# A token and memory block: x and memory loaded with channels in partitions as well, and 1/rms applied after the projections

## The reference, cut to what matters

```python
def rms_norm(x, g):
    y = xf * lax.rsqrt(jnp.mean(xf * xf, axis=-1, keepdims=True) + EPS)
    return (y * g).astype(x.dtype)

def hybrid_mixer(xn, ...):                      # xn = rms_norm(x, norm_mix)
    x_lru, g_lru, q, k, v = split(xn @ w_in)    # five times 512 columns
    xc = causal_depthwise_conv(x_lru, conv_w, conv_b)
    y_lru = rg_lru(xc, w_rg, b_rg, w_ig, b_ig, lru_lambda) * gelu(g_lru)
    y_att = attention(rope(q), rope(k), v)      # 8 heads, causal
    return concatenate([rms_norm(y_lru), rms_norm(y_att)]) @ w_out

def memory_cross_attention(hn, mem, ...):
    q = hn @ w_xq
    k, v = split(rms_norm(mem, norm_mem) @ w_xkv)
    ...
h = x + hybrid_mixer(...); h = h + memory_cross_attention(...); h = h + hier_moe(...)
```

## Time and profile before

| | us |
|---|---|
| three runs: median (lowest to highest) | 689.82 (687.18 to 691.67) |
| profiled execution: span from first to last instruction | 689.8 |
| PE busy | 551.7 (80%) |
| DVE busy | 225.3 (33%) |
| ACT busy | 168.8 (24%) |
| DMA, mean over the span | 345 GB/s |
| projections (up to the first expert) | about 0 to 240 |
| experts | about 240 to 680 |

### The profile page before, as it was taken

One profiled execution on the slowest core, in us unless ns is written; L12 is line 12 of the kernel. 1 busy time (PEld: TensorE's weight loads), 2 busy tenths in 40 slices (PEclk: granted clock), 3 DMA queues, 4 the chain that ended last, 5 costly groups with the idle time before them and its releaser, 6 DMA issues.

```text
span 689.8 us, 11578 instructions
## 1 busy us (share of the span) xinstructions
PE 551.7 (80%) x4768; PEld 346.0 (50%) x4768; DVE 225.3 (33%) x425; ACT 168.8 (24%) x325; POOL 40.1 (6%) x25
## 2 busy tenths in 40 slices
PE   3979999999999887868668767867777686767764
PEld 3968999789888644535224322522342252224221
DVE  3795888664653521222001110210120120112002
ACT  6557585463441111110000010010000000100002
POOL 2022351200000000000000000000000000000000
PEclk9989999999999999999657855976795587679557
DMA  9846743497579889999999999999999999999993
GB/s 326 289 152 211 259 152 112 156 376 265 197 293 381 313 341 409 409 410 410 410 409 409 410 410 410 409 409 410 410 410 408 410 410 410 409 409 410 410 410 139
DMA packets 75941, 237.85 MB, mean 345 GB/s; under 512 B 3728, under 2 KB 16144, under 8 KB 75920
## 3 DMA queue, kind: packets, MB, share of 16 engines
q1 hardware_dynamic: 75920, 237.56, 88.7%
HBM read 236.49 MB, written 1.05 MB: 344 GB/s over the span
## 4 chain that ended last, share of the span: by engine, by line
SPq 54%; PE 30%; issue 4%; DVE 4%; DMA 3%; POOL 1%; ACT 0%; DVEq 0%; POOLq 0%
SPq L433 53%; PE psum L562 12%; PE psum L548 8%; DMA ring<-in_w_gate_up 3%; DVE work L1259 1%; PE psum L797 1%; PE psum L822 1%; PE psum L696 1%; PE psum L719 1%; PE psum L531 1%; DVE split_w L1181 1%; PE psum L745 1%; PE psum L781 1%; POOL stat L1106 1%; PE psum L591 1%
## 5 line engine op out<-in xcount | busy, mean ns | idle before, releaser
L797 PE MATMUL psum<-ring,xg 128*32 128x256 f32 x2048 | 166.5, 468 | 61.6 <-DMA ring<-in_w_gate_up 61.0
L797 PEld LDWEIGHTS psum<-ring,xg 128*32 128x32 f32 x2048 | 66.5, 126 | 154.5 <-DMA ring<-in_w_gate_up 110.5
L562 PE MATMUL psum<-split_w,split_act 128*128 128x512 f32 x432 | 104.6, 400 | 5.4 <-DVE split_w L1181 4.2
L822 PE MATMUL psum<-ring,small 128*32 128x256 f32 x1024 | 91.6, 519 | 12.9 <-ACT small L885 11.7
L562 PEld LDWEIGHTS psum<-split_w,split_act 128*128 128x128 f32 x432 | 82.1, 192 | 23.5 <-DVE split_w L1181 4.6
L1548 DVE SCALAR_TENSOR_TENSOR small<-small,psum 128x128 f32<-128x128 f32 x32 | 9.2, 288 | 202.7 <-ACT small L1070 202.7
L1070 ACT ACTIVATE small<-psum 128x128 f32<-128x128 f32 x32 | 8.9, 277 | 268.9 <-PE psum L797 268.9
L548 PE MATMUL psum<-split_act,split_w 128*128 128x256 f32 x576 | 70.1, 284 | 1.4 <-DVE split_act L1194 1.4
L885 ACT ACTIVATE split_w<-landing 128x2048 fp32r<-128x2048 f32 x30 | 57.3, 1914 | 56.5 <-PE psum L562 32.8
L548 PEld LDWEIGHTS psum<-split_act,split_w 128*128 128x128 f32 x576 | 69.5, 192 | 2.1 <-DVE split_w L1215 1.7
L1181 DVE TENSOR_TENSOR split_w<-landing,split_w 128x2048 fp32r<-128x2048 f32 x25 | 58.9, 2360 | 29.3 <-ACT split_w L885 29.3
(11 more groups left out here) (169 smaller groups left out, 348.3 us busy)
## 6 DMA issues: line engine op xcount, KB each, us to landing
ring<-in_w_gate_up SPq DMA_DIRECT2D x128, 1024.0 KB, 18.3
ring<-in_w_down SPq DMA_DIRECT2D x64, 1024.0 KB, 18.4
landing<-in_w_in SPq DMA_DIRECT2D x10, 1024.0 KB, 9.2
landing<-in_w_xkv SPq DMA_DIRECT2D x8, 1024.0 KB, 6.3
landing<-in_w_out SPq DMA_DIRECT2D x4, 1024.0 KB, 6.8
landing<-in_w_xq SPq DMA_DIRECT2D x4, 1024.0 KB, 5.3
landing<-in_w_xo SPq DMA_DIRECT2D x4, 1024.0 KB, 5.1
res<-in_x SPq DMA_DIRECT2D x2, 512.0 KB, 3.8
```

The source lines that it names most:

```text
L562: i = mm(b, src[t][:, k0 + k, P * h:P * h + P], w[a][:, k, :], start=first and k == 0 and n == 0, stop=last and k == CT - 1 and n == 2)
L797: i = mm(half[SLOTS * strip:SLOTS * strip + SLOTS], xg[:, CT * part + k, SLOTS * j:SLOTS * j + SLOTS], w[:, k, :, P * strip:P * strip + P] ...
L822: i = mm(bank(HY)[SLOTS * strip:SLOTS * strip + SLOTS, 0:256], hidT[:, SLOTS * k:SLOTS * k + SLOTS], w[:, k, 256 * strip:256 * strip + 256 ...
```

## The change

x and memory are also passed in with channels in partitions (`x_turned`, `mem_turned`; the laying out is part of the inputs' preparation). The kernel splits them right there with the gain, before any 1/rms is known. The 1/rms is a factor of each token, so it is applied when a projection leaves PSUM: where tokens are in partitions, as the scale of the copy (`scaled`); where channels are in partitions, by a multiplication on DVE with a row `bcx` or `bcm` that holds 1/rms of all tokens in each partition (`columns_scaled`). That row is made by PE from a diagonal matrix and a matrix of ones (`broadcast`, `diagonals`). The transposes Tx and Tm are gone. Weight half 0, its split and x come in three pieces (`FIRST_CHUNKS`). The parameters stand ahead of the constants in `early` and are loaded by themselves.

```diff
-JOBS += [(f"Tx{c}", 2) for c in range(4)]
 JOBS += [(f"xl{c}", 1) for c in range(2)]
-JOBS += [(f"Tm{c}", 2) for c in range(4)]
+JOBS += [("bcx", 1)]
 JOBS += [(f"q{h}", 1) for h in range(2)] + [(f"k{h}", 1) for h in range(2)]
...
+JOBS += [("bcm", 1)]
 JOBS += [(f"xk{c}", 1) for c in range(4)]
...
+            for n, (a, b) in enumerate(FIRST_CHUNKS):
+                sp.dma_start(xraw[:, a:b], x_turned[:, a:b]).then_inc(xT_loaded[n], 16)
+                if n == 0:
+                    sp.dma_start(ctab[:, 0:N_PARAMS], early[:, 0:N_PARAMS]).then_inc(params_loaded, 16)
+                sp.dma_start(raw(0, KC)[:, a:b], half_source(0)[:, a:b]).then_inc((w_first_loaded + raw_loaded)[n], 16)
+            load_half(1)
             for h in range(NH):
                 sp.dma_start(res[:, h], x_in[:, h]).then_inc(x_loaded[h], 16)
-            sp.dma_start(ctab, early).then_inc(early_loaded, 16)
-            load_half(0)
-            load_half(1)
-            sp.dma_start(memraw, mem_in).then_inc(mem_loaded, 16)
+            sp.dma_start(ctab[:, N_PARAMS:], early[:, N_PARAMS:]).then_inc(early_loaded, 16)
             load_half(2)
+            load_half(3)
+            sp.dma_start(mraw, mem_turned).then_inc(mT_loaded, 16)
             sp.dma_start(bd.rearrange("p c n -> p (c n)"), late[:, (KC + 1) * N_ROUTES:]).then_inc(bd_loaded, 16)
-            load_half(3)
+            sp.dma_start(memtok, mem_in).then_inc(mem_loaded, 16)
             sp.dma_start(latetab, late[:, 0:(KC + 1) * N_ROUTES]).then_inc(router_loaded, 16)
...
+            w, b = slot(0, KC), begin("xl0")
+            for part, (first, last) in enumerate(FIRST_CHUNKS):
+                pe.wait_ge(x_lo, part + 1)
...
+            channels(1, "xl1", xs_)
             pe.wait_ge(early_loaded, 16)
-            pe.wait_ge(normed_act, 1)
-            pe.wait_ge(normed_dve, 1)
-            turn("Tx", xtok)
-            channels(0, "xl0", xs_, "Tx")
-            channels(1, "xl1", xs_)
-            pe.wait_ge(normed_act, 2)
-            pe.wait_ge(normed_dve, 2)
-            turn("Tm", memraw)
+            pe.wait_ge(diag_ready, 1)
+            broadcast("bcx")
             tokens_whole(2, ["q0", "q1"], xs_)
             tokens_whole(4, ["k0", "k1"], xs_)
...
-            for c in range(4):
-                await_read(pe, f"Tm{c}")
+            pe.wait_ge(diag_ready, 2)
+            broadcast("bcm")
+            pe.wait_ge(m_lo, 1)
```

ACT no longer copies gl0, gl1, xk0 and xk2 out of PSUM; it copies q, k, v, xv0 and xv2 through `scaled`:

```diff
-            plain("gl0", gx[:, 0:2])
             split_hi(12)
-            plain("gl1", gx[:, 2:4])
+            await_fill(act, "bcm")
+            release(copy(bcm, pb("bcm")[:, 0:S]), "bcm")
```

On POOL the second half of weight half 0 is gone:

```diff
             for stage in (1, 2):
                 pool.wait_ge(meansq, stage)
                 power(2 * (stage - 1), 2, rstd)
-                if stage == 1:
-                    pool.wait_ge(w_hi, 1)
-                    hi, lo = slot(0, KC)
-                    nc.gpsimd.tensor_tensor(lo[:, CT:], raw(0, KC)[:, CT:], hi[:, CT:].bitcast(F32), ALU.subtract
-                                            ).then_inc(w_lo_first, 1)
             split_lo(6)
             split_lo(8)
             split_lo(10)
```

On DVE:

```diff
+            def columns_scaled(job, dst, row):
+                await_fill(dve, job)
+                release(V.tensor_tensor(dst, pb(job).rearrange("p (c t) -> p c t", c=2),
+                                        row.unsqueeze(1).to_broadcast([P, 2, S]), ALU.mult), job)
...
             split_lo(4)
             await_read(dve, "xl0")
             await_read(dve, "xl1")
...
+            convolve(0)
+            convolve(1)
+            split_lo(5)
+            convolve(2)
+            convolve(3)
             mean_squares(2)
-            scale_half(2, memraw, memraw)
 
             dve.wait_ge(lambda_exp, 1)
...
-            split_lo(5)
-            turned_lo("Tm", ms_, "norm_mem")
+            dve.wait_ge(m_hi, 1)
+            for k in range(KC):
+                i = rest(ms_[1][:, k], mraw[:, k], param("norm_mem", k), ms_[0][:, k])
+            i.then_inc(m_lo, 1)
             split_lo(7)
+            diagonals(2)
...
             split_lo(11)
+            columns_scaled("gl0", gx[:, 0:2], bcx)
+            columns_scaled("gl1", gx[:, 2:4], bcx)
             for t in range(CT):
                 i = V.tensor_tensor_scan(xc[:, t], decay[:, t], root[:, t], 0.0, ALU.mult, ALU.add)
```

More of the change, by code:

```diff
@@ L169, with block_kernel @@
 READS_IN_A = list(_reads)
-def block_kernel(nc, x, mem, w_in, w_out, w_xq, w_xkv, w_xo, w_gate_up, w_down, norm_final, early, late, out):
+def block_kernel(nc, x, mem, x_turned, mem_turned, w_in, w_out, w_xq, w_xkv, w_xo, w_gate_up, w_down, norm_final, early, late, out):
     with ExitStack() as ctx:
@@ L571, in tokens_whole, with broadcast @@
                 tokens(m + 1, jobs, src, CT, first=False, turned=turned)
-            pe.wait_ge(early_loaded, 16)
-            pe.wait_ge(normed_act, 1)
-            pe.wait_ge(normed_dve, 1)
-            turn("Tx", xtok)
-            channels(0, "xl0", xs_, "Tx")
-            channels(1, "xl1", xs_)
-            pe.wait_ge(normed_act, 2)
-            pe.wait_ge(normed_dve, 2)
-            turn("Tm", memraw)
+            def broadcast(job):
+                b = begin(job)
+                for h in range(NH):
+                    i = mm(b[:, P * h:P * h + P], ones, diag[:, h], start=True, stop=True)
+                end(i, job)
+            w, b = slot(0, KC), begin("xl0")
+            for part, (first, last) in enumerate(FIRST_CHUNKS):
+                pe.wait_ge(x_lo, part + 1)
+                if part < 2:
+                    pe.wait_ge(w_lo_first, part + 1)
+                else:
+                    await_split(pe, 0)
+                for k in range(first, last):
+                    for c in range(2):
+                        for n, (a, t) in enumerate(((1, 0), (0, 1), (0, 0))):
+                            i = mm(b[:, 256 * c:256 * c + 256], w[a][:, k, P * c:P * c + P], xs_[t][:, k, :],
+                                   start=k == 0 and c == 0 and n == 0, stop=k == KC - 1 and n == 2, skip_group_check=True)
+            end(i, "xl0")
+            channels(1, "xl1", xs_)
+            pe.wait_ge(early_loaded, 16)
+            pe.wait_ge(diag_ready, 1)
+            broadcast("bcx")
             tokens_whole(2, ["q0", "q1"], xs_)
@@ L902, in sum_squares, with scaled @@
                     act.wait_ge(sumsq, 2 * (stage - 1) + h + 1)
[L904 to L907 removed]
+            def scaled(job, dst, col):
+                await_fill(act, job)
+                release(copy(dst, pb(job), stat[:, RS + col:RS + col + 1]), job)
             def turned_hi(prefix, dst, gain, cs=range(4)):
@@ L922, in plain @@
                 release(copy(dst, src), job)
+            hi, _ = slot(0, KC)
+            for n, (a, b) in enumerate(FIRST_CHUNKS):
+                act.wait_ge(xT_loaded[n], 16)
+                if n == 0:
+                    act.wait_ge(params_loaded, 16)
+                for k in range(a, b):
+                    i = copy(xs_[0][:, k], xraw[:, k], param("norm_mix", k))
+                i.then_inc(x_hi, 1)
+                act.wait_ge((w_first_loaded + raw_loaded)[n], 16)
+                copy(hi[:, a:b], raw(0, KC)[:, a:b]).then_inc(w_hi_first if n < 2 else w_hi, 1)
+            split_hi(1)
             for h in range(NH):
@@ L1326, in _ @@
             normalize(1, p1)
+            await_read(dve, "bcm")
+            columns_scaled("xk0", xkT[:, 0:2], bcm)
             split_lo(14)
-            plain("xk1", xkT[:, 2:4])
+            columns_scaled("xk1", xkT[:, 2:4], bcm)
             dve.wait_ge(scanned, 1)
@@ L1338, in _ @@
             i.then_inc(ylru_lo, 1)
-            plain("xk3", xkT[:, 6:8])
+            columns_scaled("xk2", xkT[:, 4:6], bcm)
+            columns_scaled("xk3", xkT[:, 6:8], bcm)
             for c in (1, 3):
```

149 lines of the change are left out of this document (84 added, 65 removed).

## The result

The kernel before takes 689.93 us (median of 4 runs, 687.18 to 691.67), the changed one **704.26 us** (701.28 to 705.67): ratio 1.0198, 95% interval 1.0155 to 1.0241. It is slower by 2%. I had said 698 with a range of 690 to 702. The sign was right, the range missed. (All ratios here are of fast runs; only in the session of "Half 5 between the rounds" does this leave anything out, three runs of the kernel before at 695.9 to 696.5 us.)

A forecast was written before the change was run, and what follows sets the result against it. PE, with DVE ahead of it, was taken to set when the fixed-length, DMA-bound expert stage starts. Terms 0.3 + 0.45 + 3.6 + 2.6 + 1.35 = +8.3 us on 689.8 gave 698 us, range 690 to 702.

The forecast's parts named there:

- the lead of the front: PE reaches half 7 about 10 us sooner, then waits 8 us for DVE; v ends 0.3 us later than before.
- The tiny instructions: 26 DVE parameter instructions, 5.2 us alone, blocked by POOL's halves 6 and 8; 20 left at 54.1 us.
- the scans are blocked: Ahead of out0, POOL's two-input steps block DVE's four scans, ending 6.7 us later; +3.6 us wait for PE.
- the expert stage keeps its length: Expert loads run at 410 GB/s whatever other engines do, so only a shift of the stage's start moves the end.
- bcm: Two full-precision matmuls of 128 columns on PE's path: +0.45 us.
- The lead survives: Rival: POOL does not hold DVE between 45 and 54 us, v ends 10.2 us ahead, 681 us; chance 0.08.
- the tiny ones or the scans pass POOL: Rival: DVE's parameter instructions (694 us, chance 0.12), scans (692, 0.13) or both (688, 0.05) are not blocked.
- half 4 lands at 31.2 us: At the front, 3072 KB more at 388 GB/s put half 4's load 8.1 us behind latetab's earlier 23.1 us.
- my third rival: First 10 MB load at 340 instead of 388 GB/s, half 4 and DVE some 3 us later: 701 us; chance 0.07.
- +1.35 us: At xo, xo0's bank is the one xpv3 leaves, so PE waits for DVE's read until 204.13 us.
- the low clock again, +2.6 us: At out0, PE's matmuls run at the low clock after its 3.6 us wait, costing 2.6 us more.
- the profiled execution's 689.8, which is also the median: Base of the sum: all terms were added to the kernel before's profiled 689.8 us, taken as its median.

The follow-up runs named there:

- Half 5 between the rounds: Kernel before with DVE splitting half 5 between the convolution's second and third round instead of behind the fourth: 687.2 us, ratio 0.9949.
- first two experiments: Changed kernel with the 26 parameter instructions moved ahead of half 4's split: 699.13 us; changed kernel with POOL's half 8 waiting for half 7's split: 701.9 us.
- The exchange of banks: Changed kernel with xo0 and xo1 swapped in the table of last banks (xo0 in 7, xo1 in 6): 702.34 us, ratio 1.0146.
- before with one edit: Kernel before with x and memory loaded twice (690.28 us), half 5 split between convolution rounds (687.2), or POOL's half 6 waiting for the convolution (687.39).
- changed with one edit: Changed kernel with parameter instructions earlier (699.13 us), POOL's half 8 later (701.9), scans ahead of gl0/gl1 (698.89), half 4 loaded earlier (703.41), or xo0/xo1 banks swapped (702.34).
- changed with all edits: Changed kernel with its five single edits combined, plus xk2's multiplication moved to where DVE waits for ylru_hi: 686.55 us, ratio to before 0.9938.
- first kind: Unchanged kernel before, executions where POOL begins half 6 ahead of the convolution's end and PE waits about 4.2 us for half 5: 691.67 and 691.69 us.
- with its order fixed either way: Kernel before with POOL's half 6 waiting for the convolution (687.39 us, 0.9953), or with half 5 split between convolution rounds (687.2 us, 0.9949).

## Why the prediction was right and where it failed

**Right, and shown:** the lead of the front is lost on DVE. The tiny instructions lie under POOL's halves 6 and 8 (first two experiments); PE waits 7.68 us in v (8 said; PE came at 57.58 instead of 55.5 and half 7 at 65.20 instead of 63.5, so two late times nearly cancel); the scans are blocked, 7.04 us (6 to 7 said); PE waits 3.69 at out0 (3.6 said); the expert stage keeps its length, so that a shift ahead of it is a shift of the last landing (9.48 and 9.53). bcm costs what was said: PE came to out0 at 115.24, that is 2.31 us later than before, of which 1.74 were there since v. "The lead survives", "the tiny ones or the scans pass POOL" did not happen.

**Mis-sized: "half 4 lands at 31.2 us".** It landed at 33.19; half 2, for which I had 18.6, at 21.07. DVE, which I had end half 7 at 63.5, ended it at 65.20, and v came 1.74 us later than before instead of 0.3. From 8 us on the DMA ran at 378 to 400 GB/s as I had assumed. In the first 8 us it moved less:

```profile
0.00:8.00 8.00, 0.00 (x0) 0.00 (x0) 1.03 (x3) 3.33 (x6) 0.30 (x5) 1.00 0.64 198
8.00:16.00 8.00, 6.47 (x32) 6.23 (x33) 4.65 (x9) 4.56 (x8) 0.00 (x0) 1.00 1.05 378
```

(windows of the changed kernel, columns as in the earlier trace rows). Before it was 260 GB/s in the first 8 us; 62 x 8 = 496 KB less are 1.3 us at 388 GB/s. That is most of the 2 us, and it is my third rival, to which I had given 0.07, in part. I had counted from the landing of latetab in the kernel before, and so had taken its first 8 us for the changed kernel's. That the small first pieces are the reason was not tried by itself.

**Mis-sized: "+1.35 us" for xo0.** The exchange of banks shows 1.95. The read by DVE was at 210.08 as worked out, but PE starts 0.25 us behind it, and before it began xo 0.35 us ahead of the end that the profile models for xpv.

**Wrong in the profile, right in most executions: "the low clock again, +2.6 us" at out0.** The first profile shows 5.70 us for 24 matmuls, no loss. Other profiles with the same wait of 3.69 to 3.70 show 7.33, 8.32, 8.22 and 7.33 us: 1.6 to 2.6 us lost. I had made one number of what is a draw.

**Put at nothing: the clock behind xo.** My sum ends at xo. Two places behind it cost 3.5 us in the profiled execution: the four matmuls at L758 ahead of the gather (3.43 us against 1.96) and the tail (20.5 against 18.5). The tail is spread: 18.5, 20.4 and 18.5 us in the three profiles of before, 20.5 and 18.3 in the two of the changed kernel. The stretch from xo's start to the gather is more than that:

| profiles | from xo's start to the gather, us |
|---|---|
| before, three | 35.32, 37.01, 35.31 |
| before with one edit, three | 35.32, 35.32, 35.31 |
| changed, two | 36.90, 38.18 |
| changed with one edit, five | 38.20, 36.87, 36.88, 38.17, 36.99 |
| changed with all edits | 35.73 |

The changed kernel is 1.6 to 2.9 us longer here than the first kind of before, 2.1 in the mean of seven profiles, and this term was missing from the sum. In its second profile the granted clock is 0.50 from 240 to 250 us; before it was that low from 232 to 234. Why the low clock falls on this stretch more often stays open: with all edits together it does so much less.

**The failed step: "the profiled execution's 689.8, which is also the median".** As a number 689.8 does fit the median run. But the terms were counted against the profiled execution, whose run took 691.67 us, the slowest of the first four. It was one of two kinds, and I took its 4.17 us wait and 8.15 us of matmuls for a property of the kernel: "before, v ended at 71.3". In the other kind the kernel before has xo 5.2 us earlier, and against that the lead is not just gone but negative.

The terms as measured, against the first kind: 1.74 (v) + 0.57 (bcm, with what lies around it) + 3.69 (out0) + 1.7 (the low clock there, mean of five profiles: 0, 1.6, 1.6, 2.5 and 2.6) + 1.95 (xo) = 9.7 us, 8.3 said; with 2.1 from xo to the gather it is 11.8. The kernel before as it runs is a mix: with its order fixed either way it is 3.2 to 3.5 us faster (0.9953 and 0.9949). If the 5.2 us between the kinds reach the end on average, it has 1.7 to 2.0 of them already; that is an estimate, since the one profile of the second kind kept only 1.4. It makes 13.5 to 13.8 us, inside the interval of the measured ratio (10.7 to 16.6 us), with the medians 14.3 apart. By size, then, the steps that failed are the clock behind xo put at nothing (2.1), one kind taken for the kernel (1.7 to 2.0) and half 4's landing (1.4 in v); the bank (0.6) came on top, and the low clock at out0 went the other way (0.9 less). The intervals of the ratios leave some 3 us either way, so the split is known only roughly.

One sum was loose as well, without effect on the forecast: 10 MB at 340 instead of 388 GB/s are 3.6 us later and not 3.

## What to carry to other kernels

A wait in one profile that hangs on which of two engines comes first by less than a us is not a property of the kernel: profile twice before making it a term, and if it is there at times only, fix the order. Fixing it was worth about as much (0.5%, by one wait or one moved split) as the whole new layout with its order mended (0.6%). When a change frees one engine, write out the queue of the next one: PE came to half 7 at 57.58 us, some 8 us sooner than before, and lost this lead behind 26 instructions of 0.16 us that had come to lie under POOL.
